# Constant products in TensorE's waits at the norms, 64-column sums, and each token's sum on all partitions

## The reference

```python
x = layer_norm(ALPHA * x + 0.5 * swiglu(x, ffn1_w_gu[l], ffn1_w_down[l]), ln1_g[l], ln1_b[l])
x = layer_norm(ALPHA * x + hybrid_mixer(x, ...), ln2_g[l], ln2_b[l])
x = layer_norm(ALPHA * x + 0.5 * swiglu(x, ffn2_w_gu[l], ffn2_w_down[l]), ln3_g[l], ln3_b[l])
```

## Time and profile before

| | |
|---|---|
| median of 3 runs | 3536.97 us (3534.82 to 3539.44) |
| profiled execution | 3536.19 us |
| its span, first to last instruction | 3534.4 us |
| PE busy | 3380.6 us, 96% of the span |
| DVE busy / ACT busy | 1781.7 us (50%) / 1330.6 us (38%) |
| mean granted TensorE clock | 0.975 |
| chain that ended last | PE 79%, DVE 11%, ACT 7% |

### The profile page before, as it was taken

The page is one execution under the profiler, slowest core; times in us unless marked ns, Lnnn a source line. Parts: engine busy times, 40 slices in busy tenths (PEclk is TensorE's granted clock), DMA queues, the critical chain, the costliest instruction groups (busy, mean ns, idle before and its releaser), DMA issues.

```text
span 3534.4 us, 38160 instructions
## 1 busy us (share of the span) xinstructions
PE 3380.6 (96%) x15620; PEld 2787.9 (79%) x15620; DVE 1781.7 (50%) x2721; ACT 1330.6 (38%) x2106; POOL 62.0 (2%) x64
## 2 busy tenths in 40 slices
PE   8999989999999999899999899999999889999998
PEld 6888767888878887678888677777888779778886
DVE  4333684533453336845334774546444665655444
ACT  3222554322242225543322454334322565434231
POOL 0000000000000000000000000000000000000000
PEclk9999999999999999989999999999999999999999
DMA  4333311333323333113333233212333313213332
GB/s 148 101 96 88 79 48 54 99 98 96 96 79 101 96 90 78 49 54 96 108 99 91 68 94 103 84 54 78 104 96 99 86 48 91 78 48 108 99 97 66
DMA packets 604286, 304.10 MB, mean 86 GB/s; under 512 B 43600, under 2 KB 601808, under 8 KB 603984
## 3 DMA queue, kind: packets, MB, share of 16 engines
q1 hardware_dynamic: 604112, 301.66, 29.8%
HBM read 299.52 MB, written 2.10 MB: 85 GB/s over the span
## 4 chain that ended last, share of the span: by engine, by line
PE 79%; DVE 11%; ACT 7%; DMA 1%; issue 1%; SPq 0%; DVEq 0%; ACTq 0%
PE ps L1613 24%; PE ps L1614 24%; PE ps L1621 24%; DVE wl L2000 2%; DVE Y L2173 1%; PE ps L1637 1%; PE ps L1630 1%; ACT wh L1785 1%; DVE tmp L2009 1%; DVE XR L2096 1%; PE ps L1671 1%; ACT XH L1827 1%; PE ps L1770 1%; PE ps L1754 1%; DVE XL L2082 1%
## 5 line engine op out<-in xcount | busy, mean ns | idle before, releaser
L1613 PE MATMUL ps<-XH,wh 128*128 128x512 f32 x2600 | 1053.4, 405 | 51.8 <-ACT XH L1827 14.6
L1621 PE MATMUL ps<-XL,wh 128*128 128x512 f32 (+1 forms) x2856 | 1066.7, 385 | 0.0
L1614 PE MATMUL ps<-XH,wl 128*128 128x512 f32 x2600 | 1027.0, 395 | 0.0
L2000 DVE TENSOR_TENSOR wl<-raw,wh 128x1024 fp32r<-128x1024 f32 (+1 forms) x565 | 680.2, 1209 | 532.3 <-ACT wh L1785 532.0
L1785 ACT ACTIVATE wh<-raw 128x1024 fp32r<-128x1024 f32 (+1 forms) x565 | 584.2, 1039 | 559.7 <-PE ps L1621 496.9
L1621 PEld LDWEIGHTS ps<-XL,wh 128*128 128x128 f32 x2856 | 545.1, 191 | 106.4
L1613 PEld LDWEIGHTS ps<-XH,wh 128*128 128x128 f32 x2600 | 498.0, 192 | 163.0 <-issue 36.4
L1614 PEld LDWEIGHTS ps<-XH,wl 128*128 128x128 f32 x2600 | 498.2, 192 | 104.1 <-issue 3.1
L1613 PE MATMUL ps<-HHa,wh 128*128 128x512 f32 x1088 | 428.9, 394 | 14.9 <-DVE HLa L2004 11.4
L1614 PE MATMUL ps<-HHa,wl 128*128 128x512 f32 x1088 | 423.9, 390 | 0.0
L1621 PE MATMUL ps<-HLa,wh 128*128 128x512 f32 x1088 | 408.1, 389 | 0.0
(11 more groups left out here) (322 smaller groups left out, 3051.9 us busy)
## 6 DMA issues: line engine op xcount, KB each, us to landing
raw<-in_ffn_w_gu SPq DMA_DIRECT2D x176, 512.0 KB, 3.8
raw<-in_w_ff SPq DMA_DIRECT2D x128, 512.0 KB, 4.1
raw<-in_ffn_w_down SPq DMA_DIRECT2D x64, 512.0 KB, 3.9
raw<-in_w_xkv SPq DMA_DIRECT2D x32, 512.0 KB, 3.9
raw<-in_ev_w_in SPq DMA_DIRECT2D x25, 512.0 KB, 3.9
raw<-in_ffn_w_down SPq DMA_DIRECT2D x32, 384.0 KB, 3.4
raw<-in_w_in SPq DMA_DIRECT2D x24, 512.0 KB, 3.9
raw<-in_w_out SPq DMA_DIRECT2D x64, 128.0 KB, 2.8
```

The costliest lines, as they stand in the source:

```text
L1613: e.matmul(bank[:, 0:n], t.wh[u % SPL][:, k, :], h, start=first, stop=False)
L1614: e.matmul(bank[:, 0:n], t.wl[u % SPL][:, k, :], h, start=False, stop=False)
L1621: m = e.matmul(bank[:, 0:n], t.wh[u % SPL][:, k, :], l, start=False, stop=last)
L2000: self.e.tensor_tensor(wl, raw, f32(wh), ALU.subtract).then_inc(self.s["lo"], self.tag("lo", f"lo.{i}"))
```

## The change

1. `finish_steps` no longer leaves the tail to TensorE: DVE adds the last tile to the sum and its square to the sum of squares (two, for RMS one, 128x512 additions), and TensorE makes 8 (RMS 4) products in place of 16 (8).
2. Each of these products has 64 columns of ones, not one; the sum is read from every 64th column. The reduction L2026 goes: DVE reads the mean's sum and the squares' from PSUM directly, and in an RMS norm ACT takes the root straight from PSUM.
3. `keep_busy`: products of a constant (`ones` by 256 columns of the constant table) into a bank that nobody reads, before the sums, after them, and after the broadcast: 3, 1 and 3 at a layer norm, 4, 1 and 4 at a post-block RMS norm, 4, 1 and 0 at the last.
4. `block_norm` (`whole=True`): the sum over features is put on all partitions by one product of `ones` with the 512-column sum tile (`p_center_sum`), so DVE forms `XR - sum/1024` first and then multiplies with rstd. mean·rstd is no longer broadcast there. `long_conv` keeps the old form.

```diff
+WIDE = 64
+BUSY_LN = (3, 1, 3)
+BUSY_RMS = (4, 1, 4)
+BUSY_LAST = (4, 1, 0)
...
+    def finish_steps(self, n, e, blocks=NB, busy=(0, 0, 0), whole=False):
         w = self.w
+        fill = [*w.psum.take(), ()] if any(busy) else None
+        w.keep_busy(fill, busy[0])
         tb, bf = w.psum.take()
-        ap, key, q, a = self.tail or (None,) * 4
-        nt = 1 if q is None else 2
+        if self.tail:
+            ap, key, q, a = self.tail
+            if self.mean:
+                x = self.first if self.k1 is None else (self.s1[:, :], self.k1)
+                self.k1 = w.sum_dve(self.s1[:, :], x[0], ap, (x[1], key, self.f1))
+            self.k2 = w.sum_dve(self.s2[:, :], self.s2[:, :], q[:, :], (a, self.k2))
+            w.tmp.give(q, self.k2)
...
+        if whole:
+            bank, bf = w.psum.take()
+            sums = w.uid("sums")
+            w.p_center_sum(sums, bank, self.s1, (self.k1, bf))
+            w.tmp.give(self.s1, sums)
         c, cf = w.st_ring.take()
         yield
         k = w.uid("rstd")
-        w.rstd(k, c, tb, nt, blocks, n, e, self.mean, (t, cf))
+        w.rstd(k, c, tb, blocks, n, e, self.mean, (t, cf))
...
+        w.keep_busy(fill, busy[1])
+        out = [(bank, sums)] if whole else []
         yield
-        for o, part in ((4, "r"), (20, "mr"))[:2 if self.mean else 1]:
+        for o, part in ((4, "r"), (20, "mr"))[:2 if self.mean and not whole else 1]:
...
+        w.keep_busy(fill, busy[2])
...
-        (rb, rt), (mb, mt) = self.stats.finish(D, LN_EPS)
+        (sb, st), (rb, rt) = self.stats.finish(D, LN_EPS, BUSY_LN, True)
...
         for b in range(blocks):
-            o = nt * (at0 + b) + i
-            m = self.e.matmul(tb[:, o:o + 1], x[:, b * P:(b + 1) * P], self.t.ones[:, 0:1], start=True, stop=True)
+            o = WIDE * (at0 + b)
+            m = self.e.matmul(tb[:, o:o + WIDE], x[:, b * P:(b + 1) * P], self.t.ones[:, 0:WIDE], start=True, stop=True)
...
+    def p_busy(self, k, bank, n, after):
+        for f in flat(after):
+            self.hold.wait_ge(*self.at(f))
+        for _ in range(n):
+            m = self.e.matmul(bank[:, 0:2 * P], self.t.ones, self.t.CT[:, 0:2 * P], start=True, stop=True)
+        m.then_inc(self.s["pe"], self.tag("pe", k))
...
-        v.tensor_reduce(c[:, 24:24 + g], tb[:, 0:nt * g].rearrange("p (g i) -> p g i", i=nt), AX, ALU.add).then_inc(
-            dve, self.tag("dve", f"{k}.read"))
...
-        self.e.tensor_tensor(q[:, :], self.t.XR[:, m, :], rb[:, :], ALU.mult).then_inc(
+        self.e.scalar_tensor_tensor(out=q[:, :], in0=sb[:, :], scalar=-1.0 / D, in1=self.t.XR[:, m, :], op0=ALU.mult,
+                                    op1=ALU.add).then_inc(
```

More of the change, by code:

```diff
@@ L242, in fold, with finish @@
         self.tail = None
-    def finish(self, n, e, blocks=NB):
-        steps = self.finish_steps(n, e, blocks)
+    def finish(self, n, e, busy=(0, 0, 0), whole=False):
+        steps = self.finish_steps(n, e, NB, busy, whole)
         while True:
@@ L270, in finish_steps @@
         k = w.uid("rstd")
-        w.rstd(k, c, tb, nt, blocks, n, e, self.mean, (t, cf))
-        w.psum.give(tb, f"{k}.read")
-        out = []
+        w.rstd(k, c, tb, blocks, n, e, self.mean, (t, cf))
+        w.psum.give(tb, f"{k}.read" if self.mean else f"{k}.sd")
+        w.keep_busy(fill, busy[1])
+        out = [(bank, sums)] if whole else []
         yield
-        for o, part in ((4, "r"), (20, "mr"))[:2 if self.mean else 1]:
+        for o, part in ((4, "r"), (20, "mr"))[:2 if self.mean and not whole else 1]:
             bank, bf = w.psum.take()
@@ L279, in finish_steps @@
         w.st_ring.give(c, t)
+        w.keep_busy(fill, busy[2])
+        if fill:
+            w.psum.give(fill[0], fill[2])
         return out
@@ L441, in sum_pool, with column_sums, keep_busy @@
         return k
-    def column_sums(self, tb, nt, at, i, blocks, x, after):
+    def column_sums(self, tb, at, blocks, x, after):
         k = self.uid("colsum")
-        self.p_column_sums(k, tb, nt, at, i, blocks, x, after)
+        self.p_column_sums(k, tb, at, blocks, x, after)
         return k
+    def keep_busy(self, fill, n):
+        if fill and n:
+            k = self.uid("busy")
+            self.p_busy(k, fill[0], n, fill[1])
+            fill[2] = k
     def broadcast(self, bank, blocks, c, o, after):
@@ L1801, in p_copy_act, with rstd @@
         self.e.activation(out, in_, ACT.Copy).then_inc(self.s["act"], self.tag("act", k))
-    def rstd(self, k, c, tb, nt, blocks, n, e, mean, after):
-        w = blocks
-        self.hold.wait_ge(*self.at(f"{k}.var" if mean else f"{k}.read"))
+    def rstd(self, k, c, tb, blocks, n, e, mean, after):
+        w, act = blocks, self.s["act"]
         if mean:
+            self.hold.wait_ge(*self.at(f"{k}.var"))
             self.e.activation(c[:, 0:w], c[:, 16:16 + w], ACT.Sqrt, bias=self.t.eps(e)).then_inc(
-                self.s["act"], self.tag("act", f"{k}.sd"))
+                act, self.tag("act", f"{k}.sd"))
         else:
-            self.e.activation(c[:, 0:w], c[:, 24:24 + w], ACT.Sqrt, bias=self.t.eps(e), scale=1.0 / n).then_inc(
-                self.s["act"], self.tag("act", f"{k}.sd"))
+            for f in flat(after):
+                self.hold.wait_ge(*self.at(f))
+            self.e.activation(c[:, 0:w], tb[:, 0 * WIDE:w * WIDE:WIDE], ACT.Sqrt, bias=self.t.eps(e), scale=1.0 / n).then_inc(
+                act, self.tag("act", f"{k}.sd"))
     def p_bn_affine(self, k, m, q, g, b, halves, x_free):
@@ L2019, in p_mul, with rstd @@
         self.e.tensor_tensor(out, a, b, ALU.mult).then_inc(self.s["dve"], self.tag("dve", k))
[L2021 removed]
+    def rstd(self, k, c, tb, blocks, n, e, mean, after):
         v, hold, w, dve = self.e, self.hold, blocks, self.s["dve"]
[L2023 removed]
+        s1, s2 = tb[:, NB * WIDE:(NB + w) * WIDE:WIDE], tb[:, 0 * WIDE:w * WIDE:WIDE]
         for f in flat(after):
             hold.wait_ge(*self.at(f))
[L2026 to L2027 removed]
         if mean:
[L2029 to L2031 removed]
+            v.tensor_scalar(c[:, 8:8 + w], s1, 1.0 / n, None, ALU.mult).then_inc(dve, self.tag("dve", f"{k}.mean"))
             hold.wait_ge(*self.own("dve"))
```

36 lines of the change are left out of this document (15 added, 21 removed).

## The result

The changed kernel takes 3509.51 us (median of 4 runs, 3508.16 to 3510.94), the kernel before took 3537.43 beside it (4 runs, 3534.82 to 3539.44): ratio 0.9925 [0.9913, 0.9938]. That is 27.9 us faster by the medians (26.5 by the ratio), of the 34.4 forecast. The profiled execution took 3509.08 us, span 3507.3, mean granted clock 0.991 (before: 3536.19, 3534.4, 0.975).

A forecast was written before the change was run, and what follows sets the result against it. PE, busy 96%, was taken to bound the kernel, losing time at norm borders and to a 1.2 GHz clock. Sum: 20.2 + 11.2 - 1.5 + 7.7 + 0.2 - 3.4 = 34.4 us gained, 3502 us; range 3492 to 3521.

The forecast's parts named there:

- The clock: At six layer norms, borders go from 72.92 to 52.7 us and dense streams behind from 107.86 to 96.6 at 2.4 GHz.
- Price of a product: One 256-column constant product on PE takes 0.43 us, so that the products fit into the waits at the norms.
- The bound of 0.6: At 0.6 us a constant product, the layer norm's middle pair costs 0.4 us a border, 2.4 us in all.
- Sums of 64 columns: PE's sums at the norms take 0.115 us a row, since 64 columns cost less than the weight load's pace.
- RMS waits: Five RMS norm borders take 7.74 us each, 38.7 against 37.21, because DVE adds before the sums: 1.5 us lost.
- RMS streams: Five dense streams behind RMS norms go from 92.21 to 84.5 us, DVE feeding a tile every 2.15 us: 7.7 gained.
- The mixers: At both mixers' ends PE goes on 1.7 us later, waiting for DVE's two additions in `long_conv`: 3.4 us lost.
- The end: At the kernel's last border the additions lose 0.5 us and a warm broadcast gains that or more: 0.2 gained.
- The reading of the waits: PE's two leading waits stand at the norms: rstd before the broadcast, and the first `XH` behind it.
- The step that failed: `pre_scale` and `memory_rms` change by 0, between 0.5 us worse and 2 better, as their sums keep their count.
- the first rival: Clock holds or half holds, but dense streams give nothing back: 18.9 us lost, 15.5 stay, 3521 us; chance 0.15.
- My bounds for later in the blocks: The forecast's own bound for places later in the blocks: shorter waits there, -6 us.

## Why the prediction was right, and where it was off

- **The clock** (72.92 to 52.7, 107.86 to 96.6): right in direction and size, and shown: without the products the streams are 22 us longer, more than the 18.4 that they had gained, and the borders 8, about half of their 16.4. Measured 54.07 and 97.25. The 1.4 us at the borders: the sums begin 0.10 us later than worked out (966.94 - 964.98 = 1.96 for 1.86), so that the broadcast is 0.14 later, and DVE's step follows 1.27 us behind it where I had 1.19. Of the rest of the borders' gain only the sum on all partitions (5.4 us) was taken out in a run. That the additions of the tail are hidden at a layer norm (the sums end at 3.96 us for 3.86 before) and what L2026 gave there are read from rows alone.
- **Price of a product**, 0.43 us: three are 1.46 with their fill and four 1.89, so one more is 0.43; right. The bound of 0.6 didn't come.
- **Sums of 64 columns** at 0.115 us a row: right (2.00 us for 16 rows, 1.10 for 8). The Trainium skill's figure in "TensorE: Matmul & The Clock Gate", section "Back-to-back issue gap", which would have given an estimated 9 us more, does not describe these products: with 1 or 64 columns the row's pace is the same 0.12 us here.
- **RMS waits**, 7.74 a border: 7.87, and 8.22 at the first (2.5 us lost for 1.5). The loss is DVE's addition, shown by taking it away. At the first, the reciprocal starts 0.45 us after the root has ended, for 0.10 at the others; it starts after 0.10 there too in the kernel with the mixers' tail on TensorE (7.87). Why, stays open.
- **RMS streams**, 84.5: 84.40. DVE leads at 2.15 us a tile as worked out.
- **The mixers**, 1.7 each: 0.98 and 1.50, 2.5 for 3.4. That it is the additions is shown; how much of it is seen depends on where the attention's last step lies, and on the clock, which fell at the second.
- **The end**, 0.2 gained: 0.0. The broadcast went from 1.74 to 1.16 us and paid for the addition, which is worth 0.68 (the end of the kernel with the RMS tails on TensorE).
- **The reading of the waits.** "Its two leading entries stand at the norms" is wrong: the list is led by a wait in the attention (17.1 us), and between the two that I named stands the one for `wl`, 16.4 us. That is the entry in which the missing gain turned up.
- **The step that failed** is "`pre_scale` and `memory_rms` have no tail, and their sums keep their count; I take 0". I asked what `pre_scale`'s own sums cost, and not who waits there once PE comes 1.6 us sooner. The term is -5.9 us. It was the first rival's mechanism, "PE now runs into tiles and weight splits that DVE has not done", which I had as all or nothing, 18.9 us for 0.15 of chance, and counted at nothing in the forecast. My bounds for later in the blocks had only shorter waits (-6); PE's waits for `wl` became more, 18 for 12. The mechanism acts behind the six streams that `pre_scale` follows; the streams of the first five layer norms, 9.0 of the 10.6 us, keep all they gained.

The total was inside the range because this term, a sixth of the 34.8 us, was smaller than the range left for it. That is room, not foresight: the range's slow end was set by the first rival.

## What to carry to other kernels

When a stretch of the critical engine gets faster, follow each other engine's chain from the same starting point to the next place where the two meet: if that chain has a fixed length and ended just in time before, the gain ends there. Work that such a chain starts with, and that depends on nothing in it (here a weight split), can go into the border's waits. Filling waits with constant products was worth 17 us here, 10 of them with only the products just ahead of the dense stretches, and 15 (8 in the traced execution) with only those ahead of and behind the sums: try the groups apart before keeping both. Adding up a tail in PSUM is cheaper than a DVE addition where DVE's result is what everybody waits for.

## What the runs showed of the hardware that was not expected

- A fallen clock can come back during work that computes nothing: in the kernel before with products alone the grant was 0.60 on the mean of the third layer norm's border, its last constant products ran at the low clock (six rows in 2.64 us, for 1.46 at the high one), and the dense stream behind them ran at 1.00 from its start, where without them it had 6 us at 0.50. Seven of the eleven places were of this kind.
- The same border doesn't always fare alike: with one-column sums two of six layer norms lost the clock, and without products behind the broadcast their streams took 16.2, 17.8 or 19.1 us. A change that works on the clock has to be counted over all places of a kernel, not read from one.
- Eight warm rows more in a broadcast of eight cost 0.89 us, where eight alone take 1.16.
